# Re-ordering the loads, projections, norms and the gating drain of a two-layer hybrid encoder

## What is computed

```python
def reference(x, ...):
    for l in range(2):
        h = rmsnorm(x, mix_norm_g[l])
        x = x + (even_mixer(h, ...) if l == 0 else odd_mixer(h, ...))
        x = x + swiglu(rmsnorm(x, ffn_norm_g[l]), w_gate[l], w_up[l], w_down[l])
    return rmsnorm(x, final_norm_g)

def even_mixer(h, ...):
    a, gate, p = split(h @ w_in)                       # 512 columns each
    ya = silu(layernorm(conv31(a * sigmoid(gate)) + conv_b, ln_g, ln_b))
    yb = einsum(window_mean(p) - p, pool_w) * pool_scale   # windows 2, 4, 8, 16
    return concat(ya, yb) @ w_out

def odd_mixer(h, ...):
    c, uv = split(h @ w_in);  u, v = split(gelu(uv))   # 512 columns each
    yc = einsum(real(fft2(c per head)), fourier_w)     # over positions and head channels
    yd = u * (spatial_w @ layernorm(v per head) + spatial_b)   # chunks of 128 positions
    return concat(yc, yd) @ w_out
```

## Time and profile before

| | us |
|---|---|
| median of 3 runs | 2949.92 (2944.89 to 2951.25) |
| the profiled execution | 2941.42 |
| its span on the slowest core, first to last instruction | 2940.2 |
| TensorE busy | 2608.1 (89%) |
| VectorE (DVE) busy | 883.0 (30%) |
| ScalarE (ACT) busy | 576.3 (20%) |
| GpSimd (POOL) busy | 368.8 (13%) |
| mean granted TensorE clock, 8 cores | 0.951 to 0.957 |

### The profile page before, as it was taken

How to read it: one execution, slowest core, us unless ns; L and a number is a source line. 1 busy time by engine, 2 the same in 40 slices (tenths; PEclk the granted TensorE clock), 3 DMA queues, 4 the chain that set the end, 5 groups by cost and what they waited for, 6 DMA issues and landing times.

```text
span 2940.2 us, 38421 instructions; the slowest of 8 cores (2929.9 to 2940.2 us)
## 1 busy us (share of the span) xinstructions
PE 2608.1 (89%) x12586; PEld 1218.2 (41%) x12704; DVE 883.0 (30%) x1313; ACT 576.3 (20%) x992; POOL 368.8 (13%) x669
## 2 busy tenths in 40 slices
PE   3798676599999999999969877877999999999998
PEld 1245522244444444444424336423444444444443
DVE  2413564321221221221212667442122112122112
ACT  2422332111111111111103114221111111111111
POOL 1100111111000000000001553111110000000000
PEclk9897689899999999999989887999999999999999
DMA  9932289956344384343472004797644443443412
GB/s 221 221 79 57 55 205 257 229 115 116 121 90 79 122 146 84 111 104 65 125 153 81 34 1 87 203 262 168 115 104 108 73 85 108 73 79 112 75 29 101
DMA packets 265149, 342.10 MB, mean 116 GB/s; under 512 B 179840, under 2 KB 192640, under 8 KB 263808
## 3 DMA queue, kind: packets, MB, share of 16 engines
q1 hardware_dynamic: 229760, 221.30, 27.3%
q0 software_dynamic: 35200, 118.35, 23.0%
HBM read 332.09 MB, written 83.89 MB: 141 GB/s over the span
## 4 chain that ended last, share of the span: by engine, by line
PE 78%; DMA 7%; DVE 6%; issue 3%; SPq 2%; POOL 2%; ACT 1%; DVEq 0%; ACTq 0%; POOLq 0%
PE ps L151 78%; DMA xin_52<-x 2%; SPq L165 2%; DMA BIG_43<-hb_16575 1%; DVE xout_16578 L412 1%; DMA BIG_43<-hb_3513 1%; DVE xout_3516 L412 1%; DVE vt_12637 L875 1%; DMA gbc_5061<-norm_g 1%; DVE bst_3041 L707 1%; POOL ssb_44 L326 0%; DVE hb_61 L334 0%; DVE BIG_43 L896 0%; DMA pwT_3026<-ev_pool_wT 0%; DMA gbc_17979<-norm_g 0%
## 5 line engine op out<-in xcount | busy, mean ns | idle before, releaser
L151 PE MATMUL ps<-BIG_43,wgu_68_16561 128*128 128x512 bf16 x2816 | 611.0, 380 | 20.0 <-DVE gT_17984 L448 14.1
L151 PEld LDWEIGHTS ps<-BIG_43,wgu_68_16561 128*128 128x128 bf16 x2816 | 275.7, 98 | 354.9 <-issue 24.9
L151 PE MATMUL ps<-BIG_43,wgu_37_4181 128*128 128x512 bf16 x1440 | 317.7, 382 | 26.2 <-DVE gT_5068 L448 20.0
L151 PE MATMUL ps<-wd_5067,gT_5068 128*128 128x512 bf16 x1376 | 304.1, 380 | 4.9 <-DMA wd_5067<-ffn_wd 3.2
L151 PE MATMUL ps<-wd_17983,gT_17984 128*128 128x512 bf16 x1376 | 302.4, 379 | 4.2 <-DMA wd_17983<-ffn_wd 2.6
L151 PE MATMUL ps<-BIG_43,wgu_46_5072 128*128 128x512 bf16 x1376 | 299.6, 379 | 0.0
L448 DVE TENSOR_TENSOR gT_17984<-tmp_17987,ps 128x512 bf16<-128x512 f32 x176 | 120.9, 688 | 462.0 <-PE ps L151 461.7
L448 DVE TENSOR_TENSOR gT_5068<-tmp_5071,ps 128x512 bf16<-128x512 f32 x176 | 120.9, 688 | 461.8 <-PE ps L151 461.6
L151 PE MATMUL ps<-w_in_53,BIG_43 128*128 128x512 bf16 x753 | 178.2, 397 | 68.9 <-DMA BIG_43<-hb_61 46.1
L151 PEld LDWEIGHTS ps<-BIG_43,wgu_37_4181 128*128 128x128 bf16 x1440 | 141.4, 98 | 200.1 <-issue 33.6
L151 PEld LDWEIGHTS ps<-wd_5067,gT_5068 128*128 128x128 bf16 x1408 | 138.2, 98 | 170.7 <-issue 5.8
(11 more groups left out here) (124 smaller groups left out, 1878.3 us busy)
## 6 DMA issues: line engine op xcount, KB each, us to landing
wgu_68_16561<-ffn_wgu POOLq DMA_DIRECT2D x88, 512.0 KB, 5.6
wgu_37_4181<-ffn_wgu POOLq DMA_DIRECT2D x45, 512.0 KB, 6.0
wgu_46_5072<-ffn_wgu POOLq DMA_DIRECT2D x43, 512.0 KB, 5.9
xin_52<-x SPq DMA_DIRECT2D x32, 512.0 KB, 5.3
xin_3515<-x SPq DMA_DIRECT2D x32, 512.0 KB, 5.0
xres<-xout_3516 SPq DMA_DIRECT2D x32, 512.0 KB, 3.5
xin_5069<-xres SPq DMA_DIRECT2D x32, 512.0 KB, 4.0
xnat<-xout_5070 SPq DMA_DIRECT2D x32, 512.0 KB, 3.1
```

What stands on the lines that cost most here:

```text
L151: ins = self.nc.tensor.matmul(o, lhsT=l, rhs=r, start=st, stop=sp)
```

## The change

It has these parts. First projections: row 0 is requested ahead of everything, rows 2 and 3 wait until the first weight block has landed and rows from 4 on until the last has; `ag` and `p_proj` alternate for all 32 tiles, with the load stage running 6 and 12 tiles ahead; the ring of pooled rows has 15 slots, is filled while projections still run, and later loads go through POOL's queue; six of eight pooling groups run before the convolution. The pooling weights are loaded and scaled early, and folded in pairs of banks. LayerNorm scaling of the second block is an ACT Identity with scale and bias from memory. `out_proj`: the scaling comes two steps after the add instead of one and stands behind the add of a later tile; buffers move. Feed-forward slots are all fetched in step 18 of the first output projection (before: three in step 13, three at the start of `ffn`). Second layer: `h_tr(16 + t)` follows `c_proj(t)`; `v_norm` is four ACT Identities and one POOL pass, the LayerNorm shift goes through a two-row bias matmul; head 0 of the Fourier mixer is computed in steps 32 to 39 of the gating loop; its buffers `A` and `Y` lie in 152 to 176 KB. The parameter `scaled` of `load_gbc` is new and no call uses it.

```diff
@@ load_w_out
-            for i in range(0, 8, 2):
+            for i in (4, 6, 0, 2):
@@ out_proj
-            run_pipeline(len(tiles), [(4, nrm.tr), (3, nrm.scale), (2, s_add), (1, s_mm), (0, s_load)], bg)
+            run_pipeline(len(tiles), [(5, nrm.tr), (2, s_add), (4, nrm.scale), (1, s_mm), (0, s_load)], bg)
@@ ffn
-            if len(W.d) < NSLOT:
-                W.open(NSLOT - len(W.d))
             W.fetch(NSLOT)
...
-                if not last and c % 2 == 1:
-                    for t in range(c // 2 * 16, c // 2 * 16 + 16):
+                if not last and c == 1:
+                    for t in range(16):
                         h_tr(t)
@@ first projections
+        k.dma(sp, [(xin[:, 0, :], T["x"][0])], writes=[d_xin[0]])
...
         def n_load(t):
-            xs_[t] = rr("xin0", 3)
-            k.dma(sp, [(xin[:, xs_[t], :], T["x"][t])], writes=[d_xin[xs_[t]]])
+            xs_[t] = rr("xin0", 4)
+            if t == 0:
+                return
+            gate = [] if t < 2 else [d_w[WP]] if t < 4 else [d_w[WG]]
+            k.dma(sp, [(xin[:, xs_[t], :], T["x"][t])], reads=gate, writes=[d_xin[xs_[t]]])
...
-        NPN = 12
+        NPN = 15
...
         jobs = [(p_proj, t) for t in range(6)]
-        for t in range(16):
+        for t in range(NT):
             jobs.append((ag, t))
-            if t + 6 < 16:
+            if t + 6 < NT:
                 jobs.append((p_proj, t + 6))
-        jobs += [(p_proj, t) for t in range(16, 32)]
...
         for fn, t in jobs:
-            while ni[0] - 6 < t or (ni[0] < 37 and ni[0] < 6 + 2 * (jobs.index((fn, t)) + 1) * 0.8):
+            while ni[0] < min(t + 6 if fn == p_proj else t + 12, NT + 2):
                 norm_step()
             fn(t)
+            if fn == ag and t == 15:
+                for i in range(8):
+                    u_tr(0, i)
+            if fn == ag and t == 25:
+                p_sb, d_p = p_ring()
+                p_nat(NPN, sp)
...
-        for tg in range(4):
+        for tg in range(6):
             for g in range(4):
                 pool_bank(tg, g)
-            p_nat(4 * tg + 3 + NPN)
+            p_nat(4 * tg + 3 + NPN, pool)
+        for g in range(4):
+            k.op(dve, lambda e: e.tensor_scalar(out=pwT[:, g, :], in0=pwT[:, g, :], scalar1=evec[:, 2, g:g + 1], ...
@@ ln_norm, second block
+                    k.op(act, lambda e: e.activation(out=vn[:, r, oo, :], in_=z[blk][:, o, :], func=AF.Identity,
+                                                     scale=rs[:, r, 0, oo:oo + 1], bias=rs[:, r, 1, oo:oo + 1]),
@@ background of the first output projection
-            if i == 13:
-                Wf.open(3)
-                Wf.fetch(3)
+            if i == 18:
+                Wf.open(NSLOT)
+                Wf.fetch(NSLOT)
@@ second layer
         for t in range(16):
             c_proj(t)
+            h_tr(16 + t)
...
         def v_norm(t):
             for h in range(4):
-                k.op(dve, lambda e: e.tensor_scalar(out=vt[:, t % 8, h * 128:(h + 1) * 128],
-                                                    in0=vt[:, t % 8, h * 128:(h + 1) * 128],
-                                                    scalar1=mv[:, r, ti, h, 0:1], scalar2=rs[:, r, ti, h:h + 1], ...
+                k.op(act, lambda e: e.activation(out=vt[:, t % 8, h * 128:(h + 1) * 128],
+                                                 in_=vt[:, t % 8, h * 128:(h + 1) * 128], func=AF.Identity,
+                                                 scale=rs[:, r, 0, ti, h:h + 1], bias=rs[:, r, 1, ti, h:h + 1]),
-            k.op(pool, lambda e: e.tensor_tensor(out=vt[:, t % 8, :], in0=vt[:, t % 8, :], in1=vln[:, 0, :], op=ALU.mult), ...
-            k.op(pool, lambda e: e.tensor_tensor(out=vn[:, t % 3, :], in0=vt[:, t % 8, :], in1=vln[:, 1, :], op=ALU.add), ...
+            k.op(pool, lambda e: e.tensor_tensor(out=vn[:, t % 3, :], in0=vt[:, t % 8, :], in1=vln[:], op=ALU.mult), ...
...
+        def f_first(n):
+            if n < 4:
+                f_s1(0, range(8 * n, 8 * n + 8, 4))
+            else:
+                f_mix(0, range(8 * (n - 4), 8 * (n - 4) + 8, 2))
...
         for i in range(NT + 8):
...
+            if i == NT:
+                A, d_A1 = k.buf("A", 152 * KB, [32, 128], BF16)
+                Y, d_Y = k.buf("Y", 160 * KB, [2, 256], BF16, 16)
             if 0 <= i - 8 < NT:
                 sv(i - 8)
+            if i >= NT:
+                f_first(i - NT)
             if 0 <= i - 6 < NT:
                 v_norm(i - 6)
...
-        f_s1(0)
-        f_mix(0)
```

More of the change, by code:

```diff
@@ L517, in build @@
         UTP = 288
[L518 to L519 removed]
+        UT, d_UT = k.buf("UT", 128 * KB, [8, UTP], BF16, 8)
+        d_UT = [k.split(d, 2) for d in d_UT]
         o = 180 * KB
@@ L736, in ln_silu, with wfold @@
                      reads=[d_VT[r], d_evec], addw=[dB[t][0] for t in range(t0, t0 + 4)])
-        pb = [(tg, g) for tg in range(4, 8) for g in range(4)]
+        def wfold():
+            for g in range(4):
+                b = k.banks(2)
+                for nh in range(2):
+                    k.mm([(ps[:, b + nh, :], pwT[:, g, :], wo[:, 4 + g, nh * 512:(nh + 1) * 512], True, True)],
+                         reads=[d_pwT, d_wo[4 + g]], writes=[psd[b + nh]])
+                for nh in range(2):
+                    evac(nh, wo[:, 4 + g, nh * 512:(nh + 1) * 512], ps[:, b + nh, :], [psd[b + nh]],
+                         **({"writes": [d_wo[4 + g]]} if nh == 0 else {"addw": [d_wo[4 + g]]}))
+        pb = [(tg, g) for tg in range(6, 8) for g in range(4)]
         for i in range(7):
@@ L747, in build @@
                 pool_bank(tg, g)
[L748 to L755 removed]
+            if i == 2:
+                wfold()
         nrm1 = Norm(1, 192 * KB, 2, 196 * KB)
@@ L833, in build @@
                      reads=[psd[b]], addw=[d_m3])
+        b = k.banks(1)
+        k.mm([(ps[0:1, b, :], onesc[:], swT[:], True, True)], reads=[d_onesc, d_swT], writes=[psd[b]])
+        k.op(act, lambda e: e.activation(out=sbrow[0:1, :], in_=ps[0:1, b, :], func=AF.Copy), reads=[psd[b]],
+             addw=[d_sbrow])
         def u_proj(tg):
@@ L927, in ev2, with f_s1 @@
             evac(nev[0] % 2, o, i, reads, writes, addw)
-        def f_s1(h):
-            for g0 in range(0, 32, 4):
+        def f_s1(h, gs=range(0, 32, 4)):
+            for g0 in gs:
                 b = k.banks(1)
@@ L937, in f_s1, with f_mix @@
                     ps[:, b, :].rearrange("p (i r j) -> p i r j", i=4, j=4), [psd[b]], [d_A[g0 // 4]])
-        def f_mix(h):
-            for b0 in range(0, 32, 2):
+        def f_mix(h, bs=range(0, 32, 2)):
+            for b0 in bs:
                 b = k.banks(1)
```

213 lines of the change are left out of this document (107 added, 106 removed).

## The result

The changed kernel takes **2802.0 us** (median of 3, 2800.6 to 2816.9) against 2949.9: a ratio of 0.9516 with a 95% interval of 0.9475 to 0.9557. The forecast was 2789, the range 2738 to 2834. The gain is 148 us where 161 were forecast.

The account below looks back on a forecast made before the run. TensorE was the chain for 78% of the span, with feed-forward layers at their floor and waits elsewhere. Terms -37 - 3 - 37 - 7 - 20 - 55 - 2 = -161 from 2949.9 gave 2789 us, range 2738 to 2834.

Parts of the forecast that it names:

- Part 1: First projections: giving each tile its dense matmuls as its row arrives, loads gated on weights, saves 37 us (25 to 45).
- its traffic takes 0.92 MB / 275 GB/s = 3.3 us: First projections: a tile's row, transposed and stored bytes need 3.3 us, so TensorE binds from about the sixth tile.
- more room: First projections: rows held back leave the transposes more room, taken as 3 us.
- sixth rival: First projections: the gate does nothing, the first tile lands as before; weak end of part 1, chance inside the forecast's 0.60.
- Part 2: Pooling and convolution: 23 us for 26 before the convolution, -3 us (-7 to +5); its 45 us at half clock stay.
- Part 3: LayerNorm and first output projection: 198 us for 235, -37 (-60 to -16); first feed-forward layer's start -7 (-9 to 0).
- What is late next is the DMA: Output projection loops: with VectorE's chain relieved, DMA sets 4.75 us a tile instead of 4.96, bounds 3.6 and 4.96.
- second rival: Output projection loops: the DMA engines are no wall, loops run near 4.0 us a tile; -46 us, 2743; chance 0.10.
- Part 4: Second layer's start: a store ahead of each transpose on SP shortens TensorE's wait for slots, -20 us (-28 to -10).
- Part 5: Spatial gating and Fourier: normalisation to ACT, one POOL pass removed, TensorE binds at 4.75 us a tile; -55 (-62 to -25).
- fourth rival: Gating stage: ACT becomes the bound through table loads between Gelu and Identity, 5.9 us a tile, 2827 us; chance 0.05.
- Part 6: Second output projection: same loop at 4.75 us a tile, 7 us for late slot fetches; -2 us (-25 to +17).

## Why the prediction was right in sum, and where its steps failed

**Part 1 (-37, came -12.9, outside its bounds).** The failed step is "its traffic takes 0.92 MB / 275 GB/s = 3.3 us". The first tile landed at 40 us, a little earlier than the 42.75 assumed. But bytes over bandwidth is a floor, and the first tiles followed at 5.5 us each, set by a chain of latencies through one in-order queue: the sixth came at 62 us, not 53. Second, "no wait on ACT" failed: behind the sixth tile TensorE waits 11.5 us on core 0, nearly all for ACT's copies behind squares whose rows were late. These two are 20 of the 24 us; no row shows the 3 us that I took for more room. I had written myself that SP holds the loads and that copies queue behind ACT's squares, and did not follow a load through both. The run with the loads first takes the waits on ACT away and leaves the late sixth tile. The sixth rival (the gate does nothing) is true by the run without it.

**Part 2 (-3, came -0.6, and -4.2 in the convolution).** A wait of 3.3 us for pooled rows stayed, in place of 9.7; their loads over POOL's queue take 6.3 us to land in the median. Leaving the half clock in place because "the gap is not smaller" was right, and the run without the gap shows the gap as the cause. What was wrong was the single number: I took 45 us from core 0, which in the kernel before had the lowest clock of the eight in 276 to 318 us (0.50; the others 0.59 to 0.94). The -4.2 is chance: on the median core the convolution takes 43.9 us before and 48.6 after.

**Part 3 (-37 and -7, came -42.5 and -4.9).** The first add came 34.9 us behind the convolution for the 37 forecast. The loop agreed by cancellation. In "What is late next is the DMA" the price failed, 4.75 us a tile: undisturbed tiles run at 3.9 us and carry 329 to 347 GB/s. That the adds would wait for transfers is right, they wait mostly for rows (44.9 of 58.6 us in the first loop, 49.8 of 66.8 in the second). LayerNorm work "hidden beside 14 us of loop" is not hidden: the first 12 tiles take 5.3 us each. The six slots cost 27.9 - 2 x 3.9 = 20 us, not 14. 12 x 5.3 + 6 x 3.8 + 27.9 + 11 x 3.9 = 157, where I had 161. The second rival (no wall, 4.0 us) had the period right: the old order alone makes 4.96. What holds the tile at 3.9, the engines or the time until a row lands, was not tried.

**Part 4 (-20, came -14.5)** lies inside its bounds (-28 to -10): TensorE still loses its clock and some 10 us to the ring of copies.

**Part 5 (-55, came -43.1).** (Its own terms, 182 for 238.7, make -57.) The loop is right: 4.77 us a tile for 4.75 (114.4 us for 24 tiles), TensorE 99% busy; before, it ran at 6.0, not 6.2. The term that was mis-sized is the drain, 36.5 us for 24, because a Fourier head in its gaps was counted at nothing; the Fourier part took 44 for 41. By the same joints the loop gave 30.6 of the 43.1 us, the drain 2.7 and the Fourier part 9.8, the head that moved into the drain. By cause, the removed POOL pass carries about 29 us and the move to ACT 2 to 3, while I had given VectorE and POOL equal weight and had read POOL's hold on VectorE as VectorE's own time; no run puts both back together, so some 11 us are assigned to neither. The fourth rival is out: the changed kernel again has four table loads in all, and an Identity takes (groups by line, core 0)

```profile
L911 ACT ACTIVATE vt_12548<-vt_12548,rs_12553 128x128 f32<-128x128 f32 x128 | 62.8, 491 | 23.4 <-DVE rs_12553 L903 14.4
```

0.49 us for the 0.46 taken. By the figures of the Trainium skill's page "ScalarE: Activation LUTs", section "What ACT_TABLE_LOAD costs", it is an estimated 479 ns, which agrees. The rule in that page's section "Rules for kernel authors", that such arithmetic belongs on VectorE, would have changed nothing that can be measured here.

**Part 6 (-2, came -19.9).** The same failed step as in part 3: 28 tiles at 4.08 us, not 4.75, are 19 us. The price of the slots, 7 us, was about right: the first three periods take 20.3 us, 8 more than three of 4.08.

On core 0 the terms were too large by 24 (part 1), 12 (part 5), 5.5 (part 4) and 4.5 us (the pooling and the layer start), and too small by 18 (part 6), 5.5 (the first loop) and 4 (the convolution): 46 against 28, and the 18 us between them are what 143 lacks of 161. The sum was near because errors of both signs met, not because the terms were known. No run isolates what brought the first add forward by 31 us on core 0, nor part 4; there the account rests on the rows alone.

## What to carry to other kernels

The time that a supply takes per tile is the length of the dependent chain divided by the transfers in flight; bytes over bandwidth is only its floor, and on an in-order queue the place of a load among stores and transposes decides it. A DMA share near 1 is no proof of a wall: look for a period that repeats to the hundredth and for the wait inside it, which is a chain. Ask what the consumer's wait ends on: TensorE stood here for a copy on ACT, and the late row was two queues away. The busy time of an instruction can be another engine's doing, so compare its runs with and without that engine beside it. Before costing a gap as free room, ask who owns the engines that the filler borrows; and a one-off instruction that waits for a late transfer belongs behind the work that doesn't need it.

## What the runs showed of the hardware

The granted clock of one short stage differed between cores that run the same program at the same moment (0.61 to 0.90 in 264 to 300 us), and one wait of TensorE of 4.3 us ahead of it decided it: without it all eight show 1.00 and agree within 0.2 us. A DMA share of 1.01 went with 257 GB/s and one of 1.09 with 329. The Trainium skill's page "Perfetto Trace Analysis", section "Identifying the Most-Contended Engine", says that with 16 engines DMA occupancy misleads and that HBM utilization is to be read in its place; that the share misleads, these two pairs agree with. A feed-forward slot of 0.5 MB cost the first output projection's loop over 3 us, in a burst or alone, where a tile with 1.3 MB of row traffic takes 3.9; in the burst of the second loop only 1.3 us a slot are to be seen. A float32 normalisation of 128 columns on VectorE took 0.35 us, and 1.11 on average where a POOL pass over 512 float32 columns overlapped it.
